# The feature sums of the seven-product blocks are spread over the start of the up projection, and the usual weight tiles lie 32 bytes further within a partition

## What is computed

```python
def conv_ffn(u, w_up, conv_w, conv_b, w_down):
    h = u @ w_up.astype(u.dtype)                      # 1024 -> 2 * 2816
    h = causal_depthwise_conv(h, conv_w, conv_b)      # three taps along the tokens
    gate, val = jnp.split(h, 2, axis=-1)
    return (jax.nn.silu(gate) * val) @ w_down.astype(u.dtype)

def reference(x, ...):
    for i in range(2):
        ...
        f = conv_ffn(rms_norm(x, norm_ffn_pre[i]), ffn_w_up[i], ffn_conv_w[i], ffn_conv_b[i], ffn_w_down[i])
        x = x + rms_norm(f, norm_ffn_post[i])
```

## Time and profile before

| | us |
|---|---|
| median of three runs | 1143.71 |
| the profiled execution, its own time | 1143.68 |
| its span in the trace | 1141.8 |
| TensorE busy | 1118.8 (98%) |
| VectorE busy | 859.4 (75%) |
| ScalarE busy | 565.1 (49%) |

### The profile page before, as it was taken

One profiled execution on the slowest core, in us unless ns is written; L12 is line 12 of the kernel. 1 busy time (PEld: TensorE's weight loads), 2 busy tenths in 40 slices (PEclk: granted clock), 3 DMA queues, 4 the chain that ended last, 5 costly groups with the idle time before them and its releaser, 6 DMA issues.

```text
span 1141.8 us, 15391 instructions
## 1 busy us (share of the span) xinstructions
PE 1118.8 (98%) x6378; PEld 971.7 (85%) x6378; DVE 859.4 (75%) x1011; ACT 565.1 (49%) x650; POOL 37.0 (3%) x93
## 2 busy tenths in 40 slices
PE   8999999999999979999999999999799999999998
PEld 7888888888888968899899888899589989988886
DVE  6778889999754886899998532699789999883235
ACT  5667676767533544444444332574444545532323
POOL 6000000000100000000000000000000000000000
PEclk9999999999999989999999999999899999999999
DMA  8244343433234113323324323512222422323321
GB/s 273 75 136 152 123 130 117 138 117 127 73 111 147 50 64 109 112 74 112 110 74 130 113 90 111 166 37 75 92 75 75 132 89 90 133 75 114 108 74 73
DMA packets 85412, 122.06 MB, mean 107 GB/s; under 512 B 4215, under 2 KB 71391, under 8 KB 85344
## 3 DMA queue, kind: packets, MB, share of 16 engines
q1 hardware_dynamic: 85162, 121.02, 31.9%
q10 hardware_dynamic: 182, 0.07, 0.0%
HBM read 118.92 MB, written 2.16 MB: 106 GB/s over the span
## 4 chain that ended last, share of the span: by engine, by line
PE 92%; DVE 5%; DMA 1%; ACT 1%; issue 1%; DVEq 0%; SPq 0%; ACTq 0%
PE bank L1075 27%; PE bank L342 18%; PE bank L344 18%; PE bank L343 18%; PE bank L550 4%; DVE t_new L1221 2%; PE bank L836 1%; DVE w_lo L312 1%; PE bank L788 1%; PE bank L827 1%; DVE tmp L569 1%; PE bank L778 1%; PE bank L466 1%; PE bank L1447 1%; DMA raw<-in_pool_w 0%
## 5 line engine op out<-in xcount | busy, mean ns | idle before, releaser
L342 PE MATMUL bank<-h_hi,w_hi 128*128 128x512 f32 (+1 forms) x856 | 315.9, 369 | 13.6 <-DVE w_lo L312 13.6
L344 PE MATMUL bank<-h_hi,w_lo 128*128 128x512 f32 (+1 forms) x856 | 312.2, 365 | 0.0
L343 PE MATMUL bank<-h_lo,w_hi 128*128 128x512 f32 (+1 forms) x856 | 312.2, 365 | 0.0
L312 DVE TENSOR_TENSOR w_lo<-raw,w_hi 128x2048 fp32r<-128x2048 f32 x90 | 206.0, 2289 | 17.4 <-ACT w_hi L307 16.2
L307 ACT ACTIVATE w_hi<-raw 128x2048 fp32r<-128x2048 f32 x90 | 171.8, 1909 | 58.4 <-PE bank L344 57.3
L342 PEld LDWEIGHTS bank<-h_hi,w_hi 128*128 128x128 f32 x856 | 162.8, 190 | 39.6 <-DVE w_lo L312 14.4
L344 PEld LDWEIGHTS bank<-h_hi,w_lo 128*128 128x128 f32 x856 | 162.6, 190 | 26.3
L343 PEld LDWEIGHTS bank<-h_lo,w_hi 128*128 128x128 f32 x856 | 162.9, 190 | 24.5
L569 DVE SCALAR_TENSOR_TENSOR tmp<-bank,par,tmp 128x511 f32<-128x511 f32 (+1 forms) x176 | 129.2, 746 | 25.5 <-ACT tmp L560 21.8
L1075 PE MATMUL bank<-w_hi,dn_hi 128*128 128x512 f32 x348 | 107.5, 390 | 0.2 <-DVE w_lo L312 0.2
L1075 PE MATMUL bank<-w_hi,dn_lo 128*128 128x512 f32 x348 | 107.3, 389 | 0.0
(11 more groups left out here) (228 smaller groups left out, 1608.1 us busy)
## 6 DMA issues: line engine op xcount, KB each, us to landing
raw<-in_ffn_w_up SPq DMA_DIRECT2D x44, 1024.0 KB, 5.0
raw<-in_ffn_w_down SPq DMA_DIRECT2D x22, 1024.0 KB, 4.8
raw<-in_ssd_w_in SPq DMA_DIRECT2D x19, 1024.0 KB, 5.2
decay<-ac_dram SPq DMA_DIRECT2D x16, 512.0 KB, 5.3
raw<-in_ssd_w_out SPq DMA_DIRECT2D x8, 1024.0 KB, 4.9
from_start<-ac_dram SPq DMA_DIRECT2D x32, 128.0 KB, 4.4
xres<-in_x SPq DMA_DIRECT2D x4, 512.0 KB, 5.7
result<-xres SPq DMA_DIRECT2D x3, 512.0 KB, 2.6
```

What stands on the lines that cost most here:

```text
L312: dve.tensor_tensor(lo[:], raw[n % 2][:], hi[:].bitcast(F32), ALU.subtract).then_inc(lo_ready, 1)
L342: pe.matmul(dst, wh, xh, start=first, stop=False, **kw)
L343: pe.matmul(dst, wh, xl, start=False, stop=False, **kw)
L344: return pe.matmul(dst, wl, xh, start=False, stop=last, **kw)
```

## The change

**Memory.** A gap of 8 numbers (32 bytes) goes ahead of the four usual weight tiles, and one of 56 numbers behind them, so that everything behind moves by 256 bytes in all.

**Order.** `combos_dve`, `combos_hi_act` and `combos_lo_dve` become `combo_dve`, `combo_hi_act` and `combo_lo_dve` for one sum each. VectorE makes the first and the second sum, each with its low part right behind it, ahead of turn 0. The third goes behind `split_lo` of U3 and the fourth behind `split_lo` of U4, both in turn 1. ScalarE's copies move with them. The instructions are the same in kind and number. `seven_pe` asks for three sums ahead of P4 and for the fourth ahead of P7.

```diff
+        sb("gap_a", [P, 8])
         w_hi = [sb(f"w_hi{s}", [P, SLAB], F32R) for s in range(2)]
         w_lo = [sb(f"w_lo{s}", [P, SLAB], F32R) for s in range(2)]
+        sb("gap_b", [P, 56])
...
-            pe.wait_ge(t_ready7, 4 * (l + 1))
+            pe.wait_ge(t_ready7, 4 * l + 3)
             seven_product(pe, P4, plain(1, 1), combo(4)).then_inc(blk_done, 1)
             pe.wait_ge(ws_ready, 2 * t + 1)
+            pe.wait_ge(t_ready7, 4 * (l + 1))
             seven_product(pe, P7, summed(0, 0), combo(3))
...
+        def combo_dve(dve, l, c):
...
+            dve.tensor_tensor(new(j), *first, ALU.subtract).then_inc(t_step, 1)
+            for k, (more, op) in enumerate(then):
+                dve.wait_ge(t_step, done + k + 1)
+                dve.tensor_tensor(new(j), new(j), more, op).then_inc(t_sum if k == len(then) - 1 else t_step, 1)
+            dve.wait_ge(t_sum, 4 * l + c + 1)
...
                 for s in range(2):
                     if i:
                         split_hi(act, n + s + 1, (f_done, 4) if l == 0 and i == 1 and s == 0 else (blk_done, base + 2 * s))
+                    if i == SEVEN0 - 1 and s == 0:
+                        combo_hi_act(act, l, 2)
                     for j in range(2):
                         up_tap_act(act, l, i, 2 * s + j)
+                        if i == SEVEN0 - 1 and s == 1 and j == 0:
+                            combo_hi_act(act, l, 3)
...
-                    if s == 0 and i == SEVEN0 - 1:
-                        combos_hi_act(act, l, [3])
...
                     if i:
                         split_lo(dve, n + s + 1)
+                    if i == SEVEN0 - 1:
+                        combo_dve(dve, l, 2 + s)
+                    if i == SEVEN0 - 1 and s == 0:
+                        combo_lo_dve(dve, l, 2)
                     for j in range(2):
                         up_taps_dve(dve, l, i, 2 * s + j)
-                    if s == 0 and i == SEVEN0 - 1:
-                        combos_lo_dve(dve, l, [3])
+                        if i == SEVEN0 - 1 and s == 1 and j == 0:
+                            combo_lo_dve(dve, l, 3)
...
-            combos_dve(dve, 0, False)
-            combos_lo_dve(dve, 0, range(3))
-            combos_dve(dve, 0, True)
+            for c in range(2):
+                combo_dve(dve, 0, c)
+                combo_lo_dve(dve, 0, c)
```

More of the change, by code:

```diff
@@ L1226, in combos_dve @@
             hi = lambda k, half: h_part(h_hi, k, half).bitcast(F32)
             lo = lambda k, half: h_part(h_lo, k, half).bitcast(F32)
-            view = lambda ap: ap.rearrange("p (k n) -> p k n", n=HALF)
+            new = lambda j: t_sums(j).rearrange("p (k n) -> p k n", n=HALF)
+            j = T_ORDER[c]
+            first, then = {1: ((hi(0, 1), hi(0, 0)), ((lo(0, 1), ALU.add), (lo(0, 0), ALU.subtract))),
+                           2: ((hi(1, 1), new(1)), ((lo(1, 1), ALU.add),)),
+                           4: ((new(2), hi(1, 0)), ((lo(1, 0), ALU.subtract),)),
+                           3: ((hi(1, 1), hi(0, 1)), ((lo(1, 1), ALU.add), (lo(0, 1), ALU.subtract)))}[j]
@@ L1229, in combos_dve @@
+            done = 6 * l + [0, 2, 3, 4][c]
             dve.wait_ge(h_ready, 8 * (1 + 2 * l) + 8)
-            if last:
-                n[0] += 4
+            if j == 3:
                 dve.wait_ge(t_ready7, 4 * l + 1)
[L1233 to L1243, removed]
+            dve.tensor_tensor(new(j), *first, ALU.subtract).then_inc(t_step, 1)
+            for k, (more, op) in enumerate(then):
+                dve.wait_ge(t_step, done + k + 1)
+                dve.tensor_tensor(new(j), new(j), more, op).then_inc(t_sum if k == len(then) - 1 else t_step, 1)
@@ L1252, in combo_view, with combo_hi_act, combo_lo_dve @@
             return tile[:, j - 1, :, :].rearrange("p k n -> p (k n)")
[L1254 to L1265, removed]
+        def combo_hi_act(act, l, c):
+            act.wait_ge(t_sum, 4 * l + c + 1)
+            act.activation(combo_view(t_hi, T_ORDER[c]), t_sums(T_ORDER[c]), ACT.Copy).then_inc(t_hi_ready, 1)
+        def combo_lo_dve(dve, l, c):
+            j = T_ORDER[c]
+            dve.wait_ge(t_hi_ready, 4 * l + c + 1)
+            dve.tensor_tensor(combo_view(t_lo, j), t_sums(j), combo_view(t_hi, j).bitcast(F32),
+                              ALU.subtract).then_inc(t_ready7, 1)
         def weights_sum_dve(dve, l, i):
@@ L1727, in _ @@
             features_act(act, 1, 3)
-            combos_hi_act(act, 0, range(3))
+            for c in range(2):
+                combo_hi_act(act, 0, c)
             up_act(act, 0, 0)
@@ L1767, in _ @@
             split_hi(act, S_UP[1] + 2)
-            combos_hi_act(act, 1, range(3))
+            for c in range(2):
+                combo_hi_act(act, 1, c)
             up_act(act, 1, 0)
@@ L1901, in _ @@
             split_lo(dve, S_UP[1] + 2)
-            combos_dve(dve, 1, False)
-            combos_lo_dve(dve, 1, range(3))
-            combos_dve(dve, 1, True)
+            for c in range(2):
+                combo_dve(dve, 1, c)
+                combo_lo_dve(dve, 1, c)
             up_dve(dve, 1, 0)
```

## The result

The changed kernel takes **1149.48 us** (median of five runs, 1149.36 to 1149.69) against 1143.71 us before (five runs, 1143.01 to 1144.38). The ratio is 1.0050, with a 95% interval of 1.0035 to 1.0065: **slower by 5.8 us**, where 1123.4 was forecast, and above the end of the range, 1133.5. The profiled execution has a span of 1147.8 us against 1141.8.

What follows compares the result with a forecast made beforehand. TensorE bounds the kernel (92% of the span), through its waits and matmul pace. 1143.7 - 10.2 (order) - 10.1 (32 bytes, after 0.8 hidden) = 1123.4 us; range 1119.0 to 1133.5.

Steps and rivals of the forecast that it cites:

- The order: VectorE's sums from U2 to U6: shorter TensorE wait ahead of U3, gaining 5.5 us in layer 0, 4.65 in layer 1.
- The 32 bytes at 256 columns: 1800 matmuls with w stationary: offset from the moving operand gains 1.7 ns each, 3.1 us.
- The 32 bytes at 512 columns: Same gain carried over: 1920 matmuls with w stationary by 1.7 ns, 3.3 us; 1440 with w moving by 3.1, 4.5 us.
- what hides: From U2 to U6 VectorE sets the pace, so 0.8 us of the matmul gain does not show.
- Slower: Rival: shift makes 512-column matmuls dearer, as next slab's copies and splits meet TensorE's reads; example 6.7 ns, 1152.9 us; chance 0.04.
- The address does nothing: Rival: wf's 1.7 ns come from something else, so only the order gains; 1133.5 us; chance 0.17.
- Works at 256 alone: Rival: the shift gains at 256 columns only, a longer stream hiding what is saved; 1130.7 us; chance 0.17.
- The clock still falls: Rival: TensorE's clock still drops in the shortened waits, costing up to 2.6 + 1.7 us; 1127.7 us; chance 0.08.
- The new order stalls more: Rival: U4's low part comes 2 to 3 us later again, order gains 5 instead of 10; 1128.6 us; chance 0.04.
- The two read ports: Skill page's rule of independent moving and stationary ports: an address would matter to nothing, second half of the sum 0.

Runs made afterwards that it cites:

- e1: The changed kernel without the two gaps: new order kept, every tile where it lay before; 1135.07 us, ratio 0.9921.
- e3: The changed kernel with the first 32-byte gap moved ahead of h_hi, so h, raw and w are shifted alike; 1142.00 us, ratio 0.9981.
- e8: The changed kernel asking for 16 bytes in gap_a; w still lies 32 bytes further, everything behind it 288, in step with w; 1142.01 us.
- e4: The changed kernel with the first gap between w_hi and w_lo, so only w_lo is 32 bytes off; 1146.44 us, ratio 1.0019.

## Why the prediction was wrong

**The order: right in mechanism and size.** Every step of VectorE's chain held within 0.3 us; the new waits for the copies (1.20 in the trace, 1.05 forecast), the wait ahead of U3 that shrinks (in e1 to 1.1 us in layer 0, 1.2 forecast, and 2.3 in layer 1, as forecast), the new one ahead of U4 (1.3 us, 1.4 forecast), and U6 5.45 and 4.6 us earlier. The gain was 9.0 instead of 10.2 us, because of the end of the program.

**The 32 bytes at 256 columns: right.** 1.3 to 1.7 ns less per matmul, now on `w` too, where 1.7 was forecast: 2.6 us instead of 3.1.

**The 32 bytes at 512 columns: the wrong step.** It reads "It is the same overhead at either width, so I let the gain go over to 512 columns; no row shows a shifted tile at that width." The term was -7.8 us (1920 by 1.7 and 1440 by 3.1). It measured +19.4 (1920 by 5.4 and 1440 by 6.3): equal overheads of 13.1 and 13.4 ns were no evidence that the address acts on them in the same way. The bound from below, "nothing", was no bound either: it came from the sign of the neighbouring rows, while no row excluded a loss.

With the right term the sum closes: 1143.7 - 9.0 + 19.4 - 2.6 = 1151.5, and the 2.0 us between that and 1149.5 are what hides behind VectorE, since TensorE's waits fall from 6.0 us in e1 to 3.9 with the slower pace. The prediction had 0.8 for what hides. What makes an offset slow the stream is not shown.

**The rivals.** "Slower" came true, with a chance of 0.04, and near a size it named (6.7 ns a long matmul). That size was half the overhead, taken as an example, so its match is luck. Its reason was not the one given there, the copies and splits of the next slab: e3 and e8 run the same copies and splits, and each product in them is at full pace or not by the offset to its partner. "The address does nothing" fell (e1 against the change: 14.4 us). "Works at 256 alone" was right about the gain and missed the loss. "The clock still falls" happened in layer 1 in six of the ten traces with the new order, the changed kernel's among them, behind idle pieces of 2.0 to 2.3 us. So the argument against it, that the clock fell only behind more than 6 us of stillness, did not hold, but its price was nothing instead of up to 4.3 us, for VectorE was the bound there. "The new order stalls more" did not happen: U4's low part starts 31.8 us behind the first sum, where 31.6 was forecast.

**The two read ports.** The page "TensorE: Matmul & The Clock Gate" of the Trainium skill says in Part 2 that TensorE has two independent read ports, by which the load of the next stationary operand takes nothing from the running matmul. What the prediction drew from it, that an address would matter to nothing, does not hold for these float32r tiles: the same instructions in the same order run at 226.7 or 233.3 ns by the offset between their two operands alone (e1, e3). Whether it is the load that slows the matmul beside it is not shown; only e4's longest step, 238 ns, beside the load of the shifted `w_lo`, speaks for it.

## What to carry to other kernels

A fast neighbour with another address is evidence for its own width and roles only: before a tile is moved because of it, price every shape of matmul that reads the tile, the commonest first, and give an unseen shape a range of both signs. Where an engine is the bound for 92% of the chain, 3% on its commonest instruction outweighs 10 us of stalls removed; so look at the pace from start to start as well as at the waits. Look up in the built program where a tile begins: the gap of 16 bytes in e8 moved `w` by 32. When two edits are made at once, run each alone: here one gains 9.0 us and the other loses 16.5, and the best kernel (1133.33 us) takes the first and a small part of the second.

## What was not expected of the hardware

- The pace of a stream of float32r matmuls depends on the offset between the stationary and the moving operand within a partition. With 512 columns: 226.7 ns at 0 and 256 bytes, 233.3 at 32, 232.5 to 232.7 at 128. With 256 columns it is the other way: 120.0 at 0, 118.3 at 32, 118.8 at 128.
- At 32 bytes the role does not matter with 512 columns: 233.3 ns with `w` stationary and with it moving (the change). The pair has to be out of step: in e8 `w` and `dn` are shifted alike and stay at 226.7, in e3 `w` and `h` do.
- With `w` stationary, one shifted operand in a round of three passes costs as much as a shift of all (700 ns a round in both); with `w` moving it costs about two thirds of it (231.3 ns on the mean, with 227.1 in e1 and 233.3 in the change).
- At 64 bytes one and the same kernel takes 1136.8 to 1146.3 us, in three groups; at 0 bytes five runs lie within 0.65 us.
- The granted clock fell from its 2.4 GHz level to the 1.2 GHz one behind idle pieces of TensorE of 2.0 to 2.3 us in six traces, and stayed up behind pieces of the same length in four.
